# Second layer's normed rows turned and split by token tile, and its output-gate projection put ahead of the narrow gate, query and key projections

## What is computed

```python
h = modulate(rms_norm_2(x, norm1_g[l]), shift1, scale1)
...
proj = h @ w_in
(q_m, k_m, v_m, o_m, i_m, f_m, c_q, c_kv, k_r, gate_pre) = jnp.split(
    proj, IN_SPLIT_POINTS, axis=-1)
qk = jax.nn.silu(causal_depthwise_conv(jnp.concatenate([q_m, k_m], axis=-1), conv_w, conv_b))
...
log_i = (i_m + igate_b).astype(jnp.float32)
log_f = jax.nn.log_sigmoid((f_m + fgate_b).astype(jnp.float32))
y_m = mlstm_chunkwise(q_m, k_m, v_m, log_i, log_f).reshape(B, S, M_V_WIDTH).astype(h.dtype)
y_m = jax.nn.sigmoid(o_m) * y_m
```

## Time and profile before

| what | us |
|---|---|
| median of 3 runs | 1639.94 |
| lowest and highest | 1638.41, 1641.69 |
| span of the profiled execution | 1638.2 |
| of it PE busy | 1520.7 |

### The profile page before, as it was taken

One profiled execution on the slowest core, in us unless ns is written; L12 is line 12 of the kernel. 1 busy time (PEld: TensorE's weight loads), 2 busy tenths in 40 slices (PEclk: granted clock), 3 DMA queues, 4 the chain that ended last, 5 costly groups with the idle time before them and its releaser, 6 DMA issues.

```text
span 1638.2 us, 21248 instructions
## 1 busy us (share of the span) xinstructions
PE 1520.7 (93%) x8362; PEld 1199.8 (73%) x8362; DVE 769.3 (47%) x1470; ACT 455.3 (28%) x722; POOL 579.8 (35%) x473
## 2 busy tenths in 40 slices
PE   6989998999999999989999999999999989887885
PEld 5978887878888888857888878775688866554442
DVE  2475656378686863238215620445313254423234
ACT  4352334242231313143323232342223121000001
POOL 2571220435454444434533144520154323312222
PEclk9998999999999999989999999999999999989997
DMA  4241110325435442313222122210043689999995
GB/s 166 91 185 49 52 52 1 111 109 212 184 155 206 167 167 103 109 52 109 104 97 71 40 78 103 90 53 23 26 166 143 259 332 353 377 397 373 394 412 200
DMA packets 37347, 260.91 MB, mean 159 GB/s; under 512 B 7280, under 2 KB 7920, under 8 KB 13184
## 3 DMA queue, kind: packets, MB, share of 16 engines
q1 hardware_dynamic: 31488, 251.13, 40.7%
q0 software_dynamic: 5760, 8.41, 1.6%
HBM read 252.69 MB, written 17.30 MB: 165 GB/s over the span
## 4 chain that ended last, share of the span: by engine, by line
PE 84%; DVE 7%; issue 4%; ACT 3%; POOL 1%; DMA 1%; DVEq 0%; SPq 0%; ACTq 0%; POOLq 0%
PE G L2090 13%; PE G L2091 13%; PE G L2092 13%; PE G L2624 4%; PE SA L2624 4%; PE SA L2090 3%; PE SA L2092 3%; PE SA L2091 3%; PE PB L2092 3%; PE PB L2091 3%; PE PB L2090 3%; PE OB L2280 2%; PE G L2132 2%; PE SA L2513 1%; PE PB L2632 1%
## 5 line engine op out<-in xcount | busy, mean ns | idle before, releaser
L753 POOL TENSOR_TENSOR wl<-raw,wh 128x512 fp32r<-128x512 f32 x356 | 479.9, 1379 | 674.5 <-ACT wh L885 669.6
L885 ACT ACTIVATE wh<-raw 128x2048 fp32r<-128x2048 f32 x90 | 172.3, 1915 | 298.7 <-PE SA L2092 153.7
L2090 PE MATMUL G<-Hh,wh 128*128 128x512 f32 x544 | 217.7, 400 | 4.6 <-DVE Yl L1837 1.6
L2091 PE MATMUL G<-Hl,wh 128*128 128x512 f32 x544 | 214.4, 394 | 0.0
L2092 PE MATMUL G<-Hh,wl 128*128 128x512 f32 x544 | 214.3, 394 | 0.0
L1593 DVE SCALAR_TENSOR_TENSOR arena<-arena,st 128x256 f32<-128x256 f32 x144 | 132.9, 923 | 5.1
L2090 PEld LDWEIGHTS G<-Hh,wh 128*128 128x128 f32 x544 | 103.8, 191 | 25.7 <-DVE Yl L1837 1.9
L2092 PEld LDWEIGHTS G<-Hh,wl 128*128 128x128 f32 x544 | 103.5, 190 | 22.6
L2091 PEld LDWEIGHTS G<-Hl,wh 128*128 128x128 f32 x544 | 103.6, 190 | 19.9
L825 POOL DMA_INDIRECT raw<-xn_rows,arena x38 | 36.8, 967 | 129.4 <-PE G L2640 104.9
L2090 PE MATMUL G<-wh,Hh 128*128 128x256 f32 x256 | 76.6, 299 | 0.0
(11 more groups left out here) (528 smaller groups left out, 3111.5 us busy)
## 6 DMA issues: line engine op xcount, KB each, us to landing
raw<-in_pieces_dram SPq DMA_DIRECT2D x91, 1024.0 KB, 4.8
arena<-in_pieces_dram SPq DMA_DIRECT2D x24, 1024.0 KB, 4.8
arena<-in_wexp_dram SPq DMA_DIRECT2D x11, 2048.0 KB
dn_w<-in_wexp_dram SPq DMA_DIRECT2D x18, 1024.0 KB, 42.0
arena<-in_wexp_dram SPq DMA_DIRECT2D x12, 1024.0 KB, 30.3
gu_y<-in_wexp_dram SPq DMA_DIRECT2D x6, 2048.0 KB
gu_z<-in_wexp_dram SPq DMA_DIRECT2D x5, 2048.0 KB
gu_h<-in_wexp_dram SPq DMA_DIRECT2D x4, 2048.0 KB
```

What stands on the lines that cost most here:

```text
L753: ins = pool.tensor_tensor(low_[:, part], whole[:, part], high[:, part], ALU.subtract)
L885: act.activation(split_pair(s)[0], wait_raw(act, sp_list[s]), ACT.Copy).then_inc(S("high_split"), 1)
L2090: pe.matmul(out, ah, bh, start=first, stop=False)
L2091: pe.matmul(out, ah, bl, start=False, stop=False)
```

## The change

The order of pieces becomes om 0, om 1, qk 0 to 3, om 2, om 3. The rows are normed tile by tile: POOL makes one reciprocal root for each tile, and DVE scales tile 0 before it adds the last block to tile 3. PE turns by token tile: each of the eight h2 groups now holds four feature blocks of one tile, first the lower four blocks of each tile, then the upper four. The first om piece needs only the lower features, so PE runs its four tiles with the transposes of the coming groups in between (`between`), and the second om piece when all upper groups are split. The lower groups are scaled and shifted by DVE (`lower_whole`) and rounded by ACT (`lower_high`); the upper ones are scaled, shifted and rounded by ACT (`upper_high`); DVE makes the rests of both (`half_low`). Since the scale and the shift of a feature are now no longer those of the whole instruction, each group takes four instructions of 128 columns. One semaphore `tables_loaded` replaces six, with the counts of `TABLES`. The diff, cut to what the text speaks of:

```diff
-    return ([("qk", j) for j in range(4)] + [("om", j) for j in range(4)] + [("vm", j) for j in range(4)]
+    return ([("om", j) for j in range(2)] + [("qk", j) for j in range(4)] + [("om", j) for j in (2, 3)] + [("vm", j) for j in range(4)]
...
-    g += [("h2", f, "v") for f in range(KT)]
+    g += [("h2", i, "va"[i // NT]) for i in range(2 * NT)]
+    g += [("om", t, "a") for t in range(4)]
...
-    g += [("om", t, "a") for t in range(8)]
+    g += [("om", t, "a") for t in range(4, 8)]
...
+        TABLES = dict(smw=16, bias=32, second_tables=64, causal=80, cos=96, chunk=112, tab3=128, final_g=144)
...
-                if p == ("om", 0):
-                    sp.wait_ge(S("rows_normed"), 2 * NT)
+                    sp.dma_start(par[:, 0:PAR2["_"][1]], par2_d).then_inc(S("tables_loaded"), 16)
+                    sp.dma_start(smw2, smw2_d).then_inc(S("tables_loaded"), 16)
+                if p == ("qk", 0):
+                    sp.wait_ge(S("act_scaled"), 2)
+                    sp.wait_ge(S("dve_scaled"), 2)
                     sp.dma_start(x_spill, X[:, :]).then_inc(S("x_spilled"), 16)
...
-            pool.wait_ge(S("ss_x"), 3)
-            rstd_of(rstd2[:, 0:3], ms2[:, 0:3], ss2[:, 0:3], 3, D).then_inc(S("rstd_x"), 1)
-            pool.wait_ge(S("ss_last"), 3)
-            rstd_of(rstd2[:, 3:4], ms2[:, 3:4], ss2[:, 3:4], 1, D).then_inc(S("rstd_x"), 1)
+            for t in range(NT):
+                if t < NT - 1:
+                    pool.wait_ge(S("ss_x"), t + 3)
+                else:
+                    pool.wait_ge(S("ss_last"), 3)
+                rstd_of(rstd2[:, t:t + 1], ms2[:, t:t + 1], ss2[:, t:t + 1], 1, D).then_inc(S("rstd_x"), 1)
...
-            squares(2, hraw2, ss2, [("down", 29), ("down", 30)])
-            norm_rows(2, hraw2, rstd2)
-            act.wait_ge(S("second_tables_loaded"), 32)
+            for t in range(NT - 1):
+                wait_freed(act, "down", 28 + t)
+                act.activation(hraw2[:, t, :], Xv[:, t, :], ACT.Square, accum_out=ss2[:, t:t + 1]).then_inc(S("ss_x"), 1)
+            for t in (1, 2):
+                act.wait_ge(S("rstd_x"), t + 3)
+                act.activation(hraw2[:, t, :], Xv[:, t, :], ACT.Copy, scale=rstd2[:, t:t + 1]).then_inc(S("act_scaled"), 1)
...
+            def lower_high(t):
+                wait_freed(act, "h2", t)
+                act.activation(Hhv[:, 0:4, t * P:(t + 1) * P], htmp[:, 0, :].rearrange("p (f n) -> p f n", f=4), ACT.Copy).then_inc(S("h2_high"), 1)
+
+            def upper_high(t):
+                b = wait_group(act, "h2", NT + t)
+                if t:
+                    act.wait_ge(S("h2_low"), NT + t)
+                for f in range(4):
+                    ins = act.activation(htmp[:, 1, f * P:(f + 1) * P], b[:, f * P:(f + 1) * P], ACT.Identity,
+                                         scale=aff1[:, 4 + f:5 + f], bias=modv[:, 0, 4 + f:5 + f])
+                free_group(ins, "h2", NT + t)
+                wait_freed(act, "h2", NT + t)
+                act.activation(Hhv[:, 4:8, t * P:(t + 1) * P], htmp[:, 1, :].rearrange("p (f n) -> p f n", f=4), ACT.Copy).then_inc(S("h2_high"), 1)
+
+            def gate_rows(half):
+                for t in range(NT):
+                    b = wait_group(act, "om", 4 * half + t)
+                    free_group(act.activation(To[:, t, half * 512:(half + 1) * 512], b[:, :], ACT.Tanh, scale=0.5), "om", 4 * half + t)
+
             act.wait_ge(S("aff_ready"), 1)
-            for f in range(KT):
-                b = wait_group(act, "h2", f)
-                ins = act.activation(Hhv[:, f, :], b[:, :], ACT.Identity, scale=aff1[:, f:f + 1], bias=modv[:, 0, f:f + 1])
-                if f % 2:
-                    own(ins)
-                    if f >= 3:
-                        wait_freed(act, "h2", f - 2)
-                    ins = act.activation(htmp[:, 1, :], Hhv[:, f, :].bitcast(F32), ACT.Identity, bias=shift_neg[:, f:f + 1])
-                ins.then_inc(S("h2_high"), 1)
-
+            lower_high(0)
+            lower_high(1)
+            high(s)
+            s += 1
+            lower_high(2)
+            lower_high(3)
+            for t in range(NT):
+                upper_high(t)
+            high(s)
+            s += 1
+            gate_rows(0)
...
+                        if i == 30:
+                            dve.wait_ge(S("rstd_x"), 3)
+                            dve.tensor_scalar(hraw2[:, 0, :], Xv[:, 0, :], rstd2[:, 0:1], None, ALU.mult).then_inc(S("dve_scaled"), 1)
...
+            def lower_whole(t):
+                b = wait_group(dve, "h2", t)
+                if t:
+                    dve.wait_ge(S("h2_low"), t)
+                for f in range(4):
+                    ins = dve.tensor_scalar(htmp[:, 0, f * P:(f + 1) * P], b[:, f * P:(f + 1) * P], aff1[:, f:f + 1], modv[:, 0, f:f + 1], ALU.mult, ALU.add)
+                free_group(ins, "h2", t)
+
+            def half_low(half, t):
+                dve.wait_ge(S("h2_high"), NT * half + t + 1)
+                fs, ts = slice(4 * half, 4 * half + 4), slice(t * P, (t + 1) * P)
+                dve.tensor_tensor(Hlv[:, fs, ts], htmp[:, half, :].rearrange("p (f n) -> p f n", f=4), Hhv[:, fs, ts].bitcast(F32),
+                                  ALU.subtract).then_inc(S("h2_low"), 1)
+
+            def tile_scaled(t):
+                dve.wait_ge(S("rstd_x"), t + 3)
+                dve.tensor_scalar(hraw2[:, t, :], Xv[:, t, :], rstd2[:, t:t + 1], None, ALU.mult).then_inc(S("dve_scaled"), 1)
+
+            lower_whole(0)
             square_last(hraw2, ss2, "down", 31)
-            dve.wait_ge(S("rstd_x"), 3)
-            dve.tensor_scalar(hraw2[:, 0, :], Xv[:, 0, :], rstd2[:, 0:1], None, ALU.mult).then_inc(S("rows_normed"), 1)
-            dve.wait_ge(S("rstd_x"), 4)
-            dve.tensor_scalar(hraw2[:, 3, :], Xv[:, 3, :], rstd2[:, 3:4], None, ALU.mult).then_inc(S("rows_normed"), 1)
-            for f in range(KT):
-                b = wait_group(dve, "h2", f)
-                dve.wait_ge(S("h2_high"), f + 1)
-                if f % 2:
-                    ins = dve.scalar_tensor_tensor(Hlv[:, f, :], b[:, :], aff1[:, f:f + 1], htmp[:, 1, :], ALU.mult, ALU.subtract)
-                else:
-                    if f >= 2:
-                        wait_freed(dve, "h2", f - 2)
-                    own(dve.tensor_scalar(htmp[:, 0, :], b[:, :], aff1[:, f:f + 1], modv[:, 0, f:f + 1], ALU.mult, ALU.add))
-                    ins = dve.tensor_tensor(Hlv[:, f, :], htmp[:, 0, :], Hhv[:, f, :].bitcast(F32), ALU.subtract)
-                free_group(ins, "h2", f)
-            wait_freed(dve, "h2", KT - 1)
+            half_low(0, 0)
+            lower_whole(1)
+            tile_scaled(3)
+            half_low(0, 1)
+            for t in (2, 3):
+                lower_whole(t)
+                half_low(0, t)
+            for t in range(NT):
+                half_low(1, t)
+            wait_freed(dve, "h2", 2 * NT - 1)
...
-            pe.wait_ge(S("rows_normed"), 2 * NT)
-            for f in range(KT):
-                transposes("h2", f, [hraw2[:, t, f * P:(f + 1) * P] for t in range(NT)])
+            def tile_turned(half, t):
+                pe.wait_ge(*((S("dve_scaled"), 1), (S("act_scaled"), 1), (S("act_scaled"), 2), (S("dve_scaled"), 2))[t])
+                transposes("h2", NT * half + t, [hraw2[:, t, (4 * half + f) * P:(4 * half + f + 1) * P] for f in range(4)])
+
+            def between(t):
+                for n in ((), (3,), (4, 5), (6, 7))[t]:
+                    tile_turned(*divmod(n, NT))
+                pe.wait_ge(S("h2_low"), t + 1)
+
+            for t in range(3):
+                tile_turned(0, t)
+            wide_rows("om", ("om", 0), 0, 0, before=between)
+            pe.wait_ge(S("h2_low"), 2 * NT)
+            wide_rows("om", ("om", 1), 0, 1)
...
-            narrow("if", SMW2["if"][0], 8, "h2")
+            narrow("if", SMW2["if"][0], 8, None)
...
-            for j in range(4):
+            for j in (2, 3):
```

More of the change, by code:

```diff
@@ L815, in _ @@
                 low(p)
-            pool.wait_ge(S("ss_x"), 4)
+            pool.wait_ge(S("ss_x"), 6)
             pool.wait_ge(S("ss_last"), 4)
@@ L1073, in _ @@
             act.activation(flog, flog, ACT.Ln, bias=1.0).then_inc(S("flog_ready"), 1)
-            for j in range(4):
-                if j:
-                    high(s)
-                    s += 1
-                half = j // 2
-                for t in range(NT if j % 2 else 0):
-                    b = wait_group(act, "om", 4 * half + t)
-                    free_group(act.activation(To[:, t, half * 512:(half + 1) * 512], b[:, :], ACT.Tanh, scale=0.5), "om", 4 * half + t)
+            high(s)
+            s += 1
+            gate_rows(1)
             act.wait_ge(S("x_spilled"), 16)
@@ L1209, in _ @@
             turned(6)
-            act.wait_ge(S("rstd_x"), 5)
+            act.wait_ge(S("rstd_x"), 7)
             for t in range(NT):
@@ L1473, in cmp_step @@
```

(11 more changed lines are left out.)

37 lines of the change are left out of this document (18 added, 19 removed).

## The result

The changed kernel takes 1650.71 us (median of 4 runs, 1649.71 to 1651.14) against 1639.18 (4 runs, 1638.02 to 1641.69) for the kernel before on the same chip: a ratio of 1.0065 with a 95% interval of 1.005 to 1.008. Its profiled execution spans 1648.9 us (run time 1650.74), 10.7 more than that of before.

What follows compares the result with a forecast made beforehand. PE, busy 1520.7 of 1638.2 us, was taken to bound the kernel. Five steps sum to 50.4 us against 43.0, 7.4 more, giving a span of 1645.6 and a time of 1647.3 us, range 1641.0 to 1652.5.

Steps and rivals of the forecast that it cites:

- Wait for the rest of om 0: From the last down multiply, PE waits 10.9 us for POOL's rest of om 0, made behind the root of tile 3.
- Om 0: First om piece takes 15.3 us: 10.9 for 48 multiplies, 2.2 for 20 transposes, 2.3 lost to low clock.
- Wait for the upper halves: Ahead of om 1, PE stands still 5.6 us while ACT and DVE make the upper groups, 3.0 us a tile.
- Om 1: Second om piece takes 13.2 us: 10.9 for multiplies and 2.3 for low clock after a gap.
- Narrow gates: Behind om 1, 24 narrow multiplies at 0.227 us with PE warm take 5.4 us; before they took 7.50.
- What follows: Behind the gates: qk 0 has 5.6 us of cover, qk 1 to 3 keep their rhythm, the small-gate-matrices gap remains.
- a later split that is late: Rival: the margin at om 2 (1.1 us) or qk 0 (5.6) goes, 3 us or more on top; chance 0.05.
- The experts took nothing up: Expert stage absorbs none of the delay; the rival, weights loaded ahead bringing the end near 1640 us, had chance 0.07.
- One sign of being wrong: The forecast is wrong if the time from the end of qk 3 to the program's end is shorter than now.
- a clock that stays low through om 0: Rival: transposes between om 0's tiles keep the clock low, 12.5 us more, 1652.4; chance 0.08.
- The rule cited from the Trainium skill: Rule against the change, for PE's transposes: full clock "doesn't engage" for a transpose; the forecast sum lets transposes wake it.
- A warm PE that never waits for the upper halves: Rival at om 0 and om 1: 1.7 us a tile, no wait, 2.7 us less, 1637.2; chance 0.08.

Runs made afterwards that it cites:

- the waits filled: Changed kernel plus idle 512-column multiplies on TensorE, 32 ahead of om 0 and 19 behind it: 1645.42 us, ratio 1.0038 to the kernel before.
- the order alone: Kernel before with only the order of pieces changed, om 0 and om 1 first; norming, turning and splitting stay by feature: 1640.36 us, ratio 1.0002.
- the second: The changed kernel run once more, unaltered: 1649.34 us, ratio 1.0062 to the kernel before.
- turned between: Kernel before with the new order of pieces, and the last three features turned between om 0's token tiles: 1638.05 us, ratio 0.9990.
- sharing them: Changed kernel with POOL's om 0 rest among the roots, and DVE making the upper halves' first pass for tiles 1 and 3: 1635.78 us, ratio 0.9981.
- the early rest: Changed kernel with POOL's four instructions for the rest of om 0 placed between the four roots: 1642.52 us, ratio 1.0019 to the kernel before.

## Why the prediction was right, step by step

The mechanism and its places were right. The steps came to 6.2 us at the end of the joint, 1.2 less than the 7.4 forecast, and the whole to 4 us more than forecast; so 4 to 5 us of the difference lie outside the steps.

1. *Wait for the rest of om 0*, 10.9 us: 10.59, counted from the last addition. POOL's rest ended it, at 717.38. The four instructions of the first lower group took 1.37 (1.4 forecast), the rest 5.81 (5.84). (By their own terms the bounds for its end were 715.0 and 717.0, not 715.2 and 716.9; nothing hangs on it.)
2. *Om 0*, 15.3: 15.37. Of the low stretch 4.2 us fell on om 0 (4.5 forecast); the other 6 lay in the wait. With the waits filled om 0 took 13.35, so half a clock cost 2.0 here (2.3 forecast).
3. *Wait for the upper halves*, 5.6: 5.16, at 2.98 a tile (3.0 forecast).
4. *Om 1*, 13.2: 12.96, and 11.05 with the waits filled: 1.9 for the low clock, not 2.3.
5. *Narrow gates*, 5.4: 5.53. The sum of the five is 49.6 against 50.4 forecast, and 43.0 before: 6.6 us more, not 7.4.
6. *What follows.* The gap by the small gate matrices stayed (1.40), but no low clock followed it, where the earlier trace rows had 6.8 us; 3.4 us at half clock now lie by the cumulated gates. Missed was a wait of 0.90 at qk 2, for POOL's rest of that piece, where the kernel before and the kernels with the order alone have none; it is a small case of the rival of a later split that is late. Together this left 6.2 us at the last copy of the cumulated gates. The experts took nothing up.

What the forecast had no term for is the clock elsewhere: 3.4 us in two far stretches, in both executions of the changed kernel. Ahead of the joint the first execution had 1.6 us more than before and the second 0.4 less. The second execution spans 1646.0 us, 0.4 from the forecast 1645.6, but that is luck: it is made of 6.0 us at the joint, 3.5 in the two stretches, and 1.6 less elsewhere.

One sign of being wrong was badly chosen. The time from the end of qk 3 to the end of the program is shorter than before (843.9 against 861.2 us), as the sign has it, but only because om 0 and om 1 (21.76 us) no longer stand in it; with them it would be 4.5 us longer.

Of the rivals, a clock that stays low through om 0 is out: from 721.6 on its multiplies took 0.23 us with twenty transposes among them, and four transposes took 0.44 us. The rule cited from the Trainium skill, page "TensorE: Matmul & The Clock Gate", section "Part 4: PE-mode transpose", is not tested by that, as multiplies stand between; but in four traces (both of before, the order alone, turned between) twelve transposes ran alone behind a wait of 4.3 us, and the clock was full after them. There the rule is not borne out. A warm PE that never waits for the upper halves is what sharing them made, at 7.2 us less than before at the joint; the forecast's 2.7 less for it kept POOL's late rest.

**Open.** By the joints alone the early rest should stand 0.9 us under the kernel before and the order alone 3.8; their medians are at 1.0019 and 1.0002. The early rest's profiled run (1639.62) was the fastest of its ten, so its trace doesn't show where the others lose. One trace of each kernel can't settle it. What sets the length of the two far stretches is open too.

## What to carry to other kernels

When a wide product is put first, its weights' last preparation must come first as well, on every engine: here one engine's fixed order cost 7 us and moving four instructions gave it back. A chain that goes round two engines over one scratch costs its sum for each tile (2.98 us here). A second buffer shortened it to the first engine's own part (2.08), and giving every other tile's first pass to the second engine took all but 0.4 us of the wait away. Earlier turning pays only if what stands between it and the first multiply (rest of the weights, roots, squares) is earlier too.

## What the runs showed of the hardware

- Stretches of half clock, of 3.4, 6.8 and 10.2 us here, come behind waits of TensorE, short ones too, but not behind each. The wait of 1.4 us by the small gate matrices had 6.8 us of it in the kernel before and none in the changed one. With 1.8 us of idle work some 290 us ahead of it, a stretch lost its 3.4 us at half clock, and with them 1.4 us of time. In these traces an edit gained or lost one to three us far from its place.
- A gap of 8.58 us filled with multiplies that nobody needs kept the clock at 1.00, and the following product at 0.227 us a step instead of 0.43.
- The same scaling of 128x1024 on DVE took 1.35 to 1.37 us in the five traces where POOL's rest of a piece ran beside all of it, 0.80 in the four where that rest began 0.2 us into it, and 0.74 to 0.75 in the five with no rest beside it.
